# One decoder step on one core: halves of gate weight tiles multiplied in pairs, a router computed by tokens, another order of the first loads, and a last norm in quarters

## The chip, the cores and the metric

The kernel runs on one core of one Trainium2 chip, in one launch. The metric is the device time in microseconds (us) of an execution; lower is better. TensorE is called PE here (and its weight loads PEld), VectorE DVE, ScalarE ACT, GpSimd POOL, SyncE SP.

## The reference

One inference step of a two-layer decoder for 272 prompt tokens (16 of them meta tokens) and 8 samples of 8 new tokens, 336 tokens in all, 1024 features, float32.

```
for l in range(2):
    z = rmsnorm(x) @ w_in[l]            # q, k, v, recurrent x and y, two merge gates
    att = window attention with sinks(q, k, v)
    xc = conv4(xr)                      # 1280 recurrent features, 16 blocks of 80
    r = sigmoid(xc_block @ w_a + b_a);  i = sigmoid(xc_block @ w_i + b_i)
    rec = RG-LRU(r, i, xc) * gelu(yr)
    x += (sigmoid(ga) * (att @ w_att_proj) + sigmoid(gr) * (rec @ w_rec_proj)) @ w_out
    x += swiglu(rmsnorm(x))             # layer 0: dense; layer 1: top 2 of 8 experts by a router
return rmsnorm(x), and the new caches and states
```

The two gates `r` and `i` multiply the 1280 features by a block-diagonal matrix of sixteen 80x80 blocks. Cut into 128x128 tiles, such a matrix has 13 tiles that aren't zero in each half of 640 features: five on the diagonal, and eight beside it, which a block reaches by crossing a tile's border. A tile beside the diagonal holds weights in its first or in its last 64 rows alone.

## The kernel before

**Split products.** Activations lie features first, in tiles of 128 features x tokens. Every large product is made of three TensorE products of reduced-precision float32 (fp32r): high weights by high activations, high by low, low by high (`three`, lines 1492 to 1494). Weights stream in chunks of eight 128x128 tiles (512 KB) by the queue of SP into a ring of four buffers `raw`; ACT (`hi`) or DVE (`hi_lo`, line 941) copies a chunk to `whi`, and DVE writes what is left to `wlo` (`lo`, line 935). A buffer is loaded again when PE has counted the chunk up in `pe_chunk`. A chunk of 24 products is `chunk`.

**Start.** PE first runs 11 filler products on zeros (line 1518, `N_WARM[0]`). `par` (gains) and the two halves of chunk 0 are loaded by ACT's queue, `x` by SP's. ACT makes `xuh` (`high`, line 567) and the halves of `whi`, DVE `xul` (`low`, line 946) and the halves of `wlo` (line 1028), in turns. POOL adds up seven sums of squares (line 411), which PE needs at the end of chunk 3 (line 1499).

**Gates.** After attention come eight chunks, a pair for each gate and half: the first chunk of a pair holds tiles for the outputs i = 0, 1, 2, the second those for 3, 4 (`GATE_IN` lists each output's input tiles). Output i is summed in PSUM bank 2+i over 360 columns. DVE meanwhile splits the next chunks (`hi_lo`) and does the last convolution (`conv(9)`); ACT takes the outputs from PSUM by a sigmoid (line 713), after a sigmoid over merge gates of its own (line 705), when `pe_chunk` says that their chunk is done. PE waits on `gate_evac` before it writes a bank again. After them come 10 chunks of the recurrent `y` (`C_Y`), 8 of the attention projection (`C_A`); there DVE has hi_lo, lo, squares, scans and copies, behind a multiplication that waits for all gate outputs (line 1171).

**Router.** In the last eight chunks of layer 1, `feature(k)` follows each chunk: one float32 product gives 64 rows (8 experts and room for the sum of squares) x 336 tokens (`wr64`, line 1691), and three transposes put the features in token order. After `feature(7)` DVE copies the logits, PE transposes them, ACT takes the norm's root (line 849), and DVE picks the experts. PE runs `keep_clock` products on data that nobody reads in the waits (`N_WARM[1:]`, line 1755). POOL gathers the first expert's rows, PE transposes them (`turn_rows`, line 1783), ACT copies them (`high_rows`), and the experts' products begin (lines 1792 to 1796).

**Last norm.** PE sums squares over features into two groups of 64 rows x 168 tokens, ACT takes the root, DVE the reciprocal, PE spreads it over 128 rows, DVE scales, SP stores.

## Time and profile before

| | |
|---|---|
| time, median of 3 runs | 1368.62 us (1368.56 to 1371.15) |
| profiled execution: its own time | 1368.22 us |
| its span | 1366.4 us |
| PE, PEld busy | 99%, 92% |
| DVE, ACT, POOL busy | 79%, 59%, 10% |
| granted TensorE clock, mean | 0.997 |

The rows below are of that one execution. Each row of a timeline gives the start, the duration, the engine, the line, the operation with its output and inputs, and in brackets how long the engine was idle before it and what ended that. "x6" means six like instructions, with their whole time. A float32 product appears as two passes.

### The profile page before, as it was taken

To read this page: it belongs to the slowest core of one execution; us is meant where nothing else is said; L and a number is where in the kernel's file an instruction comes from. 1 tells how busy PE (TensorE), PEld (TensorE's weight loads), DVE (VectorE), ACT (ScalarE), POOL (GpSimd) and SP (SyncE) were. 2 spreads that over 40 slices of the span, in tenths; PEclk is the share of its full clock that TensorE was granted. 3 is DMA by queue.
4 is the path that set the end of the run, shared out by engine and by line. 5 is a ranking of instruction groups with operands and counts; after the bars stand their busy time and mean duration, and the time that the engine had idled before them with its cause. 6 is when DMAs were issued, how large, how long until landed. Compare 5 with 4: busy or idle time off the path is not lost.

```text
span 1366.4 us, 23816 instructions
## 1 busy us (share of the span) xinstructions
PE 1349.9 (99%) x8300; PEld 1251.7 (92%) x8300; DVE 1079.2 (79%) x1641; ACT 808.6 (59%) x1215; POOL 139.2 (10%) x137
## 2 busy tenths in 40 slices
PE   8999999999999999999999999999999999999997
PEld 8999999999999999999989999987888888888886
DVE  5869988876666664456699899758999999999987
ACT  5455668325333333343666584257888888888885
POOL 3200003002000000001000030022012022022010
PEclk9999999999999999999999999999999999999999
DMA  6533344445444444444423444497999999999991
GB/s 240 165 128 99 109 144 148 146 140 175 153 138 143 146 142 139 144 141 148 157 94 108 144 150 151 158 363 301 409 396 396 399 383 376 397 386 375 398 348 57
DMA packets 83401, 298.31 MB, mean 218 GB/s; under 512 B 9584, under 2 KB 10864, under 8 KB 83312
## 3 DMA queue, kind: packets, MB, share of 16 engines
q1 hardware_dynamic: 77472, 277.73, 57.2%
q0 software_dynamic: 5408, 18.72, 4.6%
q8 instruction: 57, 0.93, 0.3%
q10 hardware_dynamic: 432, 0.66, 0.1%
q14 instruction: 32, 0.26, 0.1%
HBM read 285.50 MB, written 11.58 MB: 217 GB/s over the span
## 4 chain that ended last, share of the span: by engine, by line
PE 90%; DVE 7%; ACT 2%; issue 1%; DMA 0%; ACTq 0%; DVEq 0%
PE ps L1492 19%; PE ps L1494 18%; PE ps L1493 18%; PE ps L1792 10%; PE ps L1796 10%; PE ps L1793 10%; DVE wlo L935 1%; PE ps L1828 1%; PE ps L1592 1%; DVE mx L1097 1%; ACT sp L627 1%; DVE sp L1093 1%; DVE xc L1074 1%; DVE sp L1108 0%; PE ps L1608 0%
## 5 line engine op out<-in xcount | busy, mean ns | idle before, releaser
L935 DVE TENSOR_TENSOR wlo<-raw,whi 128x1024 fp32r<-128x1024 f32 x231 | 285.7, 1238 | 122.0 <-ACT whi L549 113.8
L1014 DVE TENSOR_TENSOR mwlo<-mraw,mwhi 128x1024 fp32r<-128x1024 f32 x290 | 343.9, 1222 | 30.0 <-ACT mwhi L549 25.2
L549 ACT ACTIVATE mwhi<-mraw 128x1024 fp32r<-128x1024 f32 x290 | 304.3, 1061 | 60.6 <-PE ps L1796 55.9
L549 ACT ACTIVATE whi<-raw 128x1024 fp32r<-128x1024 f32 (+1 forms) x207 | 216.9, 1050 | 193.2 <-DMA raw<-w_mix 118.9
L1492 PE MATMUL ps<-xuh,whi 128*128 128x336 f32 x576 | 183.7, 319 | 2.5 <-DVE wlo L1028 2.0
L1493 PE MATMUL ps<-xul,whi 128*128 128x336 f32 x576 | 182.0, 316 | 0.0
L1494 PE MATMUL ps<-xuh,wlo 128*128 128x336 f32 x576 | 181.7, 315 | 0.0
L1492 PE MATMUL ps<-xnh,whi 128*128 128x336 f32 (+1 forms) x544 | 174.0, 320 | 1.9 <-DVE wlo L935 1.8
L1494 PE MATMUL ps<-xnh,wlo 128*128 128x336 f32 (+1 forms) x544 | 170.7, 314 | 0.0
L1493 PE MATMUL ps<-xnl,whi 128*128 128x336 f32 (+1 forms) x544 | 170.6, 314 | 0.0
L1792 PE MATMUL ps<-mwhi,xeh 128*128 128x512 f32 x384 | 152.7, 398 | 0.4 <-ACT xeh L549 0.4
L1796 PE MATMUL ps<-mwhi,xel 128*128 128x512 f32 x384 | 149.9, 390 | 0.0
L1793 PE MATMUL ps<-mwlo,xeh 128*128 128x512 f32 x384 | 149.6, 390 | 0.0
L1492 PEld LDWEIGHTS ps<-xuh,whi 128*128 128x128 f32 x576 | 108.7, 189 | 3.3 <-DVE wlo L1028 2.3
L1493 PEld LDWEIGHTS ps<-xul,whi 128*128 128x128 f32 x576 | 108.9, 189 | 0.3
L1492 PEld LDWEIGHTS ps<-xnh,whi 128*128 128x128 f32 x544 | 102.2, 188 | 7.4 <-issue 5.7
L1494 PEld LDWEIGHTS ps<-xuh,wlo 128*128 128x128 f32 x576 | 108.8, 189 | 0.0
L1493 PEld LDWEIGHTS ps<-xnl,whi 128*128 128x128 f32 x544 | 102.4, 188 | 0.0
L1494 PEld LDWEIGHTS ps<-xnh,wlo 128*128 128x128 f32 x544 | 102.2, 188 | 0.0
L1796 PEld LDWEIGHTS ps<-mwhi,xel 128*128 128x128 f32 x384 | 72.1, 188 | 15.8 <-DVE xel L1413 0.4
L1792 PEld LDWEIGHTS ps<-mwhi,xeh 128*128 128x128 f32 x384 | 72.2, 188 | 14.5 <-issue 0.6
L1793 PEld LDWEIGHTS ps<-mwlo,xeh 128*128 128x128 f32 x384 | 72.2, 188 | 14.0
(323 smaller groups left out, 2621.7 us busy)
## 6 DMA issues: line engine op xcount, KB each, us to landing
mraw<-w_moe SPq DMA_DIRECT2D x292, 512.0 KB, 8.1
raw<-w_mix SPq DMA_DIRECT2D x159, 512.0 KB, 3.6
raw<-w_ffn SPq DMA_DIRECT2D x72, 512.0 KB, 3.5
x<-x_in SPq DMA_DIRECT2D x4, 336.0 KB, 5.4
tok_d<-xt POOLq DMA_DIRECT2D x6, 224.0 KB, 4.3
ysum_d<-zero POOLq DMA_DIRECT2D x3, 448.0 KB, 10.7
ysum<-ysum_d POOLq DMA_DIRECT2D x3, 448.0 KB, 10.5
o_y<-nt SPq DMA_DIRECT2D x8, 168.0 KB, 1.9
```

Source lines behind the costliest of these rows:

```text
L549: return nc.scalar.activation(out, in_, ACT.Copy)
L627: nc.scalar.activation(sp[q][:, i * w:(i + 1) * w], sp[q][:, i * w:(i + 1) * w], ACT.Exp, bias=neg[q][:, i:i + 1], accum_out=rsum[q][:, i: ...
L935: v.tensor_tensor(wlo[c % RING][:, :, :], raw[c % RING][:, :].rearrange("p (k n) -> p k n", n=P), f32(whi[c % RING][:, :, :]), ALU.subtrac ...
L1014: v.tensor_tensor(mwlo[q % MRING][:, :, :], mraw[q % MRING][:, :].rearrange("p (k n) -> p k n", n=512), f32(mwhi[q % MSPLIT][:, :, :]), AL ...
L1074: step(v.scalar_tensor_tensor(out=xc[:, t, :], in0=ext[:, t, j:j + C], scalar=w[:, KR * j + t:KR * j + t + 1], in1=xc[:, t, :], op0=ALU.mu ...
L1093: ins = v.scalar_tensor_tensor(out=sp[q][:, g * per:(g + 1) * per], in0=ps[2 + 2 * q + g][:, 0:per], scalar=HD ** -0.5, in1=mask[:, 0:per] ...
L1492: mm(out, wh, xh, start=start, stop=False)
L1493: mm(out, wh, xl, start=False, stop=False)
L1494: return mm(out, wl, xh, start=False, stop=stop)
L1792: mm(out, lhs_h, hi[:, n, :], start=start, stop=False)
L1793: mm(out, lhs_h, lo[:, n, :], start=False, stop=False)
L1796: return mm(out, lhs_l, hi[:, n, :], start=False, stop=stop)
```

## The change

The gates: each pair of chunks is now one block. The five diagonal tiles are multiplied as before (`gate_in`). The eight tiles beside the diagonal are multiplied over 64 rows each (`gate_edges`), in turns one on rows 0 to 63 and one on rows 64 to 127, into different banks. A pair's first chunk is counted up in `pe_chunk` three pairs of half products before the second. The start: half a chunk, the first tile of `x`, the other half and the second tile go first on SP's queue; ACT takes a root (and so loads its table) before anything arrives; chunk 1 is split by halves. The router: `by_tokens` makes the tokens the rows, with 9 columns for each third of the tokens, in place of the 64-row product, so that the copy and the transposes of the logits fall away. The first expert's rows are copied by ACT ahead of one weight chunk. The filler counts change. The last norm works on four groups of 32 rows x 84 tokens.

```diff
-N_WARM = (11, 7, 3, 20)
+N_WARM = (11, 15, 7, 16)
...
+GATE_SLOT = {(i, k): n for part in ((0, 1, 2), (3, 4)) for n, (i, k) in enumerate((i, k) for i in part for k in GATE_IN[i])}
...
-            for q in range(4):
+            sy.dma_start(raw[0][:, 0:512], w_mix[0, 0, :, 0:512]).then_inc(raw_half, 16)
+            sy.dma_start(x[:, 0:1, :], x_in[:, 0:1, :]).then_inc(x_first, 16)
+            sy.dma_start(raw[0][:, 512:CH], w_mix[0, 0, :, 512:CH]).then_inc(raw_loaded[0], 16)
+            sy.dma_start(x[:, 1:2, :], x_in[:, 1:2, :]).then_inc(x_loaded[0], 16)
+            for q in range(1, 4):
                 sy.dma_start(x[:, 2 * q:2 * q + 2, :], x_in[:, 2 * q:2 * q + 2, :]).then_inc(x_loaded[q], 16)
...
-            def first_hi(h):
-
-                act.wait_ge(raw_half if h == 0 else raw_loaded[0], 16)
-                copy(whi[0][:, 4 * h:4 * h + 4, :], raw[0][:, 512 * h:512 * h + 512].rearrange("p (k n) -> p k n", n=P))\
+            def first_hi(c, h):
+
+                act.wait_ge(raw_half if c == 0 and h == 0 else raw_loaded[c], 16)
+                copy(whi[c][:, 4 * h:4 * h + 4, :], raw[c][:, 512 * h:512 * h + 512].rearrange("p (k n) -> p k n", n=P))\
                     .then_inc(hi_half if h == 0 else hi_done, 1)
 
             act.dma_start(par[:, :, :], par_in).then_inc(par_loaded, 16)
-            act.dma_start(raw[0][:, 0:512], w_mix[0, 0, :, 0:512]).then_inc(raw_half, 16)
-            act.dma_start(raw[0][:, 512:CH], w_mix[0, 0, :, 512:CH]).then_inc(raw_loaded[0], 16)
+            act.wait_ge(eps_set, 1)
+            nc.scalar.activation(rms3[:, 0:1], eps[:, :], ACT.Sqrt)
+            first_hi(0, 0)
             high(0, 0)
-            first_hi(0)
             high(0, 1)
-            first_hi(1)
+            first_hi(0, 1)
             for k in range(2, KD):
                 high(0, k)
-            hi(1)
+            first_hi(1, 0)
+            first_hi(1, 1)
             square(0, 0)
             square(0, 1)
             hi(2)
...
-                    for q in range(N_NEXT, LEAD):
-                        mhi(q, r)
+                    mhi(N_NEXT, r)
+                    mhi(N_NEXT + 1, r)
                     high_rows(0, 0, r)
                     high_rows(0, 1, r)
+                    for q in range(N_NEXT + 2, LEAD):
+                        mhi(q, r)
...
-            nc.scalar.activation(esg[:, 0:T // 2], ps[0][:, 0:T // 2], ACT.Sqrt, bias=eps[:, :], scale=1.0 / D).then_inc(rms_done, 1)
+            nc.scalar.activation(esg[:, 0:T // 4], ps[0][:, 0:T // 4], ACT.Sqrt, bias=eps[:, :], scale=1.0 / D).then_inc(rms_done, 1)
...
+            first_lo(0, 0)
             low(0, 0)
-            first_lo(0)
             low(0, 1)
-            first_lo(1)
+            first_lo(0, 1)
             for k in range(2, KD):
                 low(0, k)
-            lo(1)
+            first_lo(1, 0)
+            first_lo(1, 1)
...
-            ve.wait_ge(router_mm, 1)
-            v.tensor_copy(lgt[0:9, :], ps[7][0:9, 0:T]).then_inc(logits_t, 1)
...
-                for j in range(N_G):
-                    c = c0 + C_G + j
-                    half, part, pair = j // 4, j % 2, j // 2
+                def gate_in(c, i, k, half, start=False, stop=False):
+
+                    slot = GATE_SLOT[i, k]
+                    return three(ps[2 + i][:, 0:C], whi[c % RING][:, slot, :], wlo[c % RING][:, slot, :], xch[:, 5 * half + k, :],
+                                 xcl[:, 5 * half + k, :], start, stop)
+
+                def gate_edges(low, high, half):
+
+
+                    for n in range(3):
+                        for rows, (c, i, k, start, stop) in ((slice(0, 64), low), (slice(64, P), high)):
+                            slot, t = GATE_SLOT[i, k], 5 * half + k
+                            w, xin = (wlo if n == 2 else whi)[c % RING], xcl if n == 1 else xch
+                            ins = mm(ps[2 + i][:, 0:C], w[rows, slot, :], xin[rows, t, :], start=start and n == 0, stop=stop and n == 2)
+                    return ins
+
+                for pair in range(N_G // 2):
+                    c, half = c0 + C_G + 2 * pair, pair // 2
                     pe.wait_ge(lo_done, c + 1)
-                    slot = 0
-                    for i in ((3, 4) if part else (0, 1, 2)):
-                        pe.wait_ge(xc_split, KR * l + 5 * half + GATE_IN[i][-1] + 1)
+                    for i in range(3):
+                        pe.wait_ge(xc_split, KR * l + 5 * half + i + 1)
                         if pair:
                             pe.wait_ge(gate_evac, 20 * l + 5 * (pair - 1) + i + 1)
-                        for k in GATE_IN[i]:
-                            t = 5 * half + k
-                            ins = three(ps[2 + i][:, 0:C], whi[c % RING][:, slot, :], wlo[c % RING][:, slot, :], xch[:, t, :],
-                                        xcl[:, t, :], k == GATE_IN[i][0], k == GATE_IN[i][-1])
-                            slot += 1
-                    ins.then_inc(pe_chunk, 1)
+                        gate_in(c, i, i, half, start=True)
+                    pe.wait_ge(lo_done, c + 2)
+                    pe.wait_ge(xc_split, KR * l + 5 * half + 5)
+                    gate_edges((c, 0, 1, False, True), (c, 1, 0, False, False), half)
+                    if pair:
+                        pe.wait_ge(gate_evac, 20 * l + 5 * (pair - 1) + 4)
+                    gate_edges((c, 2, 3, False, False), (c + 1, 3, 2, True, False), half).then_inc(edges_mm, 1)
+                    gate_in(c + 1, 3, 3, half)
+                    if pair:
+                        pe.wait_ge(gate_evac, 20 * l + 5 * pair)
+                    gate_in(c + 1, 4, 4, half, start=True)
+                    pe.wait_ge(edges_mm, N_G // 2 * l + pair + 1)
+                    gate_edges((c, 1, 2, False, True), (c, 2, 1, False, True), half).then_inc(pe_chunk, 1)
+                    gate_edges((c + 1, 3, 4, False, True), (c + 1, 4, 3, False, True), half).then_inc(pe_chunk, 1)
...
+                def by_tokens(features, weights, stop=False):
+
+                    for t in range(NT):
+                        ins = mm(ps[7][0:TR, 9 * t:9 * t + 9], features[:, TR * t:TR * t + TR], weights, start=False, stop=stop and t == NT - 1)
+                    return ins
+
                 def feature(k):
 
+                    if k == 0:
+                        mm(ps[7][0:TR, 0:9 * NT], zero[:, 0:TR], zero[:, 0:9 * NT], start=True, stop=False)
                     pe.wait_ge(x_added, 16 + k + 1)
-                    mm(ps[7][0:64, 0:T], wr64[:, k, :], x[:, k, :], start=k == 0, stop=False)
+                    by_tokens(x[:, k, :], wr9[:, k, :])
...
-            mm(ps[7][0:64, 0:T], e64[:, :], acc3[:, :], start=False, stop=False)
+            by_tokens(acc3[:, :], e9[:, :])
             feature(KD - 1)
             pe.wait_ge(sq_done, KD * 4)
-            mm(ps[7][0:64, 0:T], e64[:, :], ssq[(KD - 1) % 2][:, :], start=False, stop=True).then_inc(router_mm, 1)
-            pe.wait_ge(tok_a, NT)
-            pe.wait_ge(logits_t, 1)
-            for t in range(NT):
-                ins = nc.tensor.transpose(ps[3][0:TR, 9 * t:9 * t + 9], lgt[0:9, TR * t:TR * t + TR], ident[0:9, 0:9])
-            ins.then_inc(logits_mm, 1)
+            by_tokens(ssq[(KD - 1) % 2][:, :], e9[:, :], stop=True).then_inc(logits_mm, 1)
...
-                for h in range(2):
-                    ins = mm(ps[0][64 * h:64 * h + 64, 0:T // 2], ones[:, 0:64], sq[:, k, T // 2 * h:T // 2 * h + T // 2],
+                for h in range(4):
+                    ins = mm(ps[0][32 * h:32 * h + 32, 0:T // 4], ones[:, 0:32], sq[:, k, T // 4 * h:T // 4 * h + T // 4],
                              start=k == 0, stop=k == KD - 1)
...
-            for h in range(2):
-                ins = mm(ps[1][:, T // 2 * h:T // 2 * h + T // 2], ident[:, 64 * h:64 * h + 1].to_broadcast([P, P]), rstd[:, 0:T // 2], start=True, stop=True)
+            for h in range(4):
+                ins = mm(ps[1][:, T // 4 * h:T // 4 * h + T // 4], ident[:, 32 * h:32 * h + 1].to_broadcast([P, P]), rstd[:, 0:T // 4], start=True, stop=True)
```

The data, `wr9` and `e9` (9 columns in place of 64), and the ring stay otherwise as they are.

ACT's first instructions, before and then after the change (`raw0` is the first ring buffer, `rms3` takes the early root):

```order
L588 DMA par_191<-par_in 128x264
L589 DMA raw0_50<-w_mix 128x512
L590 DMA raw0_50<-w_mix 128x512
L567 ACT_TABLE_LOAD [waits par_loaded]
L567 ACTIVATE xuh_92<-x_49,par_191 128x336 [waits x_loaded0]
L549 ACTIVATE whi0_58<-raw0_50 128x512 [waits raw_half]
L567 ACTIVATE xuh_92<-x_49,par_191 128x336 [waits x_loaded0]
L549 ACTIVATE whi0_58<-raw0_50 128x512 [waits raw_loaded0]
```

```order
L594 DMA par_190<-par_in 128x264
L596 ACT_TABLE_LOAD
L596 ACTIVATE rms3_242<-eps_206 128x1 [waits eps_set]
L555 ACTIVATE whi0_58<-raw0_50 128x512 [waits raw_half]
L573 ACTIVATE xuh_92<-x_49,par_190 128x336 [waits par_loaded,x_first]
L573 ACTIVATE xuh_92<-x_49,par_190 128x336 [waits x_loaded0]
L555 ACTIVATE whi0_58<-raw0_50 128x512 [waits raw_loaded0]
L573 ACTIVATE xuh_92<-x_49,par_190 128x336 [waits x_loaded1] x2
```

The table load no longer stands behind the wait for `par`, and the first half of `whi` stands ahead of the first `xuh`.

PE in the second pair of gate chunks of layer 0, before (the outputs i = 1 and the first tile of i = 2) and then after the change (from the diagonal tile of i = 2 on):

```order
L1492 MATMUL ps3<-xch_73,whi2_60 128x360 [waits gate_evac,xc_split]
L1493 MATMUL ps3<-xcl_74,whi2_60 128x360
L1494 MATMUL ps3<-xch_73,wlo2_56 128x360
L1492 MATMUL ps3<-xch_73,whi2_60 128x360
L1493 MATMUL ps3<-xcl_74,whi2_60 128x360
L1494 MATMUL ps3<-xch_73,wlo2_56 128x360
L1492 MATMUL ps3<-xch_73,whi2_60 128x360
L1493 MATMUL ps3<-xcl_74,whi2_60 128x360
L1494 MATMUL ps3<-xch_73,wlo2_56 128x360
L1492 MATMUL ps4<-xch_73,whi2_60 128x360 [waits gate_evac,xc_split]
```

```order
L1498 MATMUL ps4<-xch_73,whi2_60 128x360 [waits gate_evac,xc_split]
L1499 MATMUL ps4<-xcl_74,whi2_60 128x360
L1500 MATMUL ps4<-xch_73,wlo2_56 128x360
L1661 MATMUL ps2<-xch_73,whi2_60 128x360 [waits xc_split,lo_done]
L1661 MATMUL ps3<-xch_73,whi2_60 128x360
L1661 MATMUL ps2<-xcl_74,whi2_60 128x360
L1661 MATMUL ps3<-xcl_74,whi2_60 128x360
L1661 MATMUL ps2<-xch_73,wlo2_56 128x360
L1661 MATMUL ps3<-xch_73,wlo2_56 128x360
L1661 MATMUL ps4<-xch_73,whi2_60 128x360 [waits gate_evac]
L1661 MATMUL ps5<-xch_73,whi3_61 128x360
```

The products of line 1661 take 64 rows each and alternate between two banks; the wait for the pair's second chunk (`lo_done`) now stands behind nine products instead of 24.

PE at the end of the router, before and then after the change (`acc3` and `ssq1` are sums of squares, `xg` the scaled features):

```order
L1742 MATMUL ps7<-acc3_186,e64_180 64x336 [waits acc_done]
L1691 MATMUL ps7<-x_49,wr64_179 64x336 [waits x_added]
L1696 MATMUL ps5<-cst_190,xg1_183 112x128 [waits xg_done]
L1696 MATMUL ps6<-cst_190,xg1_183 112x128
L1696 MATMUL ps2<-cst_190,xg1_183 112x128
L1745 MATMUL ps7<-ssq1_95,e64_180 64x336 [waits sq_done]
L1749 MATMUL ps3<-cst_190,lgt_178 112x9 [waits logits_t,tok_a]
L1749 MATMUL ps3<-cst_190,lgt_178 112x9 x2
L1755 MATMUL ps1<-mwhi0_154,onesr_239 128x512 [waits x_added]
```

```order
L1719 MATMUL ps7<-e9_179,acc3_185 112x9 [waits acc_done]
L1719 MATMUL ps7<-e9_179,acc3_185 112x9 x2
L1719 MATMUL ps7<-wr9_178,x_49 112x9 [waits x_added]
L1719 MATMUL ps7<-wr9_178,x_49 112x9 x2
L1732 MATMUL ps5<-cst_189,xg1_182 112x128 [waits xg_done]
L1732 MATMUL ps6<-cst_189,xg1_182 112x128
L1732 MATMUL ps2<-cst_189,xg1_182 112x128
L1719 MATMUL ps7<-e9_179,ssq1_95 112x9 [waits sq_done]
L1786 MATMUL ps1<-mwhi0_154,onesr_238 128x512 [waits x_added]
```

Three products of 9 columns stand where one of 336 stood, and the transposes of `lgt` are gone.

## Rows read from the trace of the kernel before

**Rows 1.** The page: engines busy, and DMA in 40 slices.

```profile
PE 1349.9 (99%) x8300; PEld 1251.7 (92%) x8300; DVE 1079.2 (79%) x1641; ACT 808.6 (59%) x1215; POOL 139.2 (10%) x137
DMA  6533344445444444444423444497999999999991
```

**Rows 2.** The timeline of the first 25 us.

```profile
4.94 1.28 ACT L567 ACT_TABLE_LOAD   x1 [4.94 <-DMA par<-par_in]
7.40 0.68 DVE L1028 TENSOR_TENSOR wlo<-raw,whi 128x512 fp32r<-128x512 f32 x1
9.20 2.96 DVE L946 SCALAR_TENSOR_TENSOR xul<-x,par,xuh 128x336 fp32r<-128x336 f32 x6
9.81 0.65 PE L1492 MATMUL ps<-xuh,whi 128*128 128x336 f32 x1 [0.47 <-DVE xul L946]
14.50 8.71 POOL L411 TENSOR_TENSOR acc<-acc,ssq 128x336 f32<-128x336 f32 x6
24.71 0.73 PE L1499 MATMUL ps<-acc,cst 128*128 128x336 f32 x2
```

**Rows 3.** Windows: busy PE, PEld, DVE, ACT, POOL, granted clock, DMA.

```profile
10.00:12.00 2.00, 2.00 (x8) 2.00 (x9) 2.00 (x5) 2.00 (x4) 1.05 (x2) 0.50 1.04 423
173.13:198.85 25.72, 25.72 (x160) 25.72 (x157) 22.27 (x28) 15.82 (x28) 0.00 (x0) 1.00 0.51 151
198.90:265.10 66.20, 66.20 (x432) 66.20 (x431) 60.28 (x86) 45.72 (x67) 14.81 (x11) 1.00 0.47 151
```

**Rows 4.** The timeline of PE: attention scores, products over 64 rows.

```profile
79.20 0.31 PE L1494 MATMUL ps<-xnh,wlo 128*128 128x336 f32 x1
79.45 0.72 PE L1563 MATMUL ps<-qkx 64*128 64x128 f32 x8
80.35 0.32 PE L1493 MATMUL ps<-xnl,whi 128*128 128x336 f32 x1
116.21 1.14 PE L1568 MATMUL ps<-qkx 64*128 64x256 f32 x8
```

**Rows 5.** The timeline of DVE in the gates, layers 0 and 1.

```profile
182.41 0.69 DVE L941 CAST whi<-raw 128x1024 fp32r<-128x1024 f32 x1
200.23 2.03 DVE L1171 TENSOR_TENSOR ig<-ig,xc 128x1800 f32<-128x1800 f32 x1 [1.62 <-ACT ig L713]
768.33 0.69 DVE L941 CAST whi<-raw 128x1024 fp32r<-128x1024 f32 x1
785.13 2.03 DVE L1171 TENSOR_TENSOR ig<-ig,xc 128x1800 f32<-128x1800 f32 x1 [1.68 <-ACT ig L713]
```

**Rows 6.** The timeline of ACT at the gates' end, layer 0.

```profile
198.06 0.77 ACT L705 ACTIVATE gates<-gates 128x672 f32<-128x672 f32 x1
199.18 1.01 ACT L713 ACTIVATE ig<-ps,par 128x360 f32<-128x360 f32 x2 [0.35 <-PE ps L1494]
```

**Rows 7.** The loads of `raw` between 165 and 230 us.

```profile
DMA to landing us min/median/max: 3.4/3.5/3.9
```

**Rows 8.** The timeline in the attention projection: DVE layer 0, PE layer 1.

```profile
237.35 1.23 DVE L935 TENSOR_TENSOR wlo<-raw,whi 128x1024 fp32r<-128x1024 f32 x1
823.07 0.41 PE L1492 MATMUL ps<-atth,whi 128*128 128x320 f32 x1 [0.37 <-DVE wlo L935]
```

**Rows 9.** The timeline from the router's end to the first expert.

```profile
920.74 0.73 PE L1691 MATMUL ps<-x,wr 128*64 128x336 f32 x2
921.98 1.57 ACT L549 ACTIVATE xt<-ps 112x512 f32<-112x512 f32 x3 [1.45 <-PE ps L1696]
933.67 0.86 PEld L1783 LDWEIGHTS ps<-cst,xe 128*128 128x128 f32 x8 [0.41 <-DMA xe<-tok_d,idx]
934.45 1.06 ACT L549 ACTIVATE xeh<-ps 128x512 fp32r<-128x512 f32 x2
```

**Rows 10.** The timeline of the last norm.

```profile
1356.16 1.28 ACT L911 ACT_TABLE_LOAD   x1
1357.99 1.20 DVE L1480 RECIPROCAL rstd<-esg 128x168 f32<-128x168 f32 x1 [2.24 <-ACT esg L911]
```

43 lines of the change are left out of this document (21 added, 22 removed).

## The prediction

> **What bounds the kernel now.** I read the page first: PE is busy 99% of the span [rows 1]. So a saving must shorten PE's stream or end one of its few waits, and what is saved elsewhere is hidden. Then I read the timeline stage by stage at the five places touched.
>
> At the start PE waits for data: `par` lands at 4.94 and ACT then loads a table for 1.28 before it does anything; the first chunk's third tile starts at 9.81, released by DVE's `xul`, and PE is then at half clock [rows 2, 3]. In the gates, 25.72 hold 156 products, 0.165 each, without a wait; the 18 chunks after them take 66.20, 3.68 a chunk or 0.153 a product of 336 columns [rows 3]. Close behind PE runs DVE: in the projection after the gates it ends a `wlo` at 237.35 + 1.23 = 238.58, and PE, 11 chunks after 198.90, takes it at 198.90 + 40.46 = 239.36, only 0.8 later. In layer 1 PE does wait there, 0.37 [rows 3, 8]. So behind the gates a gain of PE lasts only as far as DVE comes earlier too. That sets the main term.
>
> **The start.** The table load moves under the load of `par`, and the first half of `whi` can be ready when `par` lands. DVE can start at about 4.95 instead of 6.92, which is 9.81 less the 2.9 of its five steps (xul and wlo in turns). PE's third tile comes at about 7.85 instead of 9.81. Two more things follow. PE's idle time between the fillers and the first product shrinks, so I take it that the clock isn't lowered; DVE's 0.49 a tile (2.96 for 6) then paces the chunk: its eighth tile at 7.85 + 5 x 0.49 = 10.3, its end at 10.8. By halves, chunk 1 starts 0.68 after DVE's last `xul`, at 11.1. Before, chunk 1 must have started at 24.71 - 2 x 3.68 - 3.22 = 14.1. That would be 3.0. But POOL's seven sums take 7 x 1.45 = 10.1 and can't start before two squares on ACT, at about 11.7: PE gets them at 21.9 instead of at 24.71, 2.8 earlier [rows 2, 3]. What hides SP's three more DMA issues is that bytes, not issues, set the landings. Term: **-2.8**. Bounds: -1.3, if the clock falls as before; -3.2.
>
> **The gates on PE.** A pair of chunks had 39 products. Now 15 are whole and 24 are halves. Do two halves run side by side? The scores have such a pattern in float32: eight passes of 64 rows and 256 columns end within 1.14 [rows 4]. A float32 pass of 336 columns takes about 0.28 (two in 0.73, the last with its tail [rows 9]), so 256 take 0.21, and eight in a row would take 1.7. They run in pairs. The switch costs: from 79.20 + 0.153 to 80.35 - 0.153 are 0.84 for eight passes of 128 columns, which in pairs need 4 x 0.107 = 0.43; 0.42 remain for a way there and back [rows 4]. A pair of chunks has two such ways: 15 x 0.165 + 12 x 0.165 + 0.84 = 5.30 instead of 6.43. Four pairs would save 4.5 a layer.
>
> The Trainium skill, "TensorEngine Tiling (Array Packing)", Key Properties, says that a change of tiling mode drains TensorE. By that rule there is a cost beside the saved products, and the trace agrees (0.42).
>
> **The gates on DVE.** DVE isn't moved by this. In layer 0 it starts `whi` of the third pair's first chunk at 182.41, 9.28 after the gates' start at 173.13, and needs 0.7 + 1.23 for the two steps: ready at 11.2. PE would be there at 10.7, so it waits 0.5. The pair's second chunk follows 1.9 later, at 13.1, but PE asks for it after nine products, at 12.7: 0.4 more. The third pair ends at 16.9, the fourth, whose chunks (freed at 10.2 and 10.8, 3.5 to land [rows 7]) are split by 15.9 and 17.8, at 22.35. PE ends the gates 25.7 - 22.35 = 3.35 earlier [rows 3, 5].
>
> Behind that: `pe_chunk` of a pair's first chunk now comes near the pair's end, so after the last pair ACT still has three outputs, the merge sigmoid and two outputs (5 x 0.45 + 0.77, less 0.3 that lie before PE's end: 2.75) instead of two outputs (1.3) [rows 6]. DVE's multiplication starts at 22.35 + 2.75 = 25.1 instead of 27.1 [rows 5]: DVE moves by 1.9 only. With its 0.8 lead less a few tenths in later chunks, PE keeps about **-2.5** in layer 0.
>
> In layer 1 the multiplication at 785.13 stands, as in layer 0, 27.1 after the gates' start, which is then 758.0; the `whi` step at 768.33 is 10.3 after it, a microsecond later than in layer 0 [rows 5]. By the same steps the gates end at 23.35, DVE's multiplication starts at 26.1 instead of 27.1 after the start, and PE has no lead to spend (it waits already [rows 8]): **-0.9**. Together **-3.4**. Bounds: -1.8, if a switch costs 0.6; -5.0 at 0.2.
>
> **The router.** A 64-row product of two passes took 0.73 with its tail, about 0.66 of PE's time [rows 9]. `by_tokens` issues three products of two passes; their columns are few, so six weight loads set the price: 0.103 each by [rows 9] (0.86 for 8), 0.064 by the 64-row passes of [rows 4] (0.72 for 8, less the tail). I take 0.48, between: 0.18 saved for each of features 0 to 5, less a zero product, is 0.9. At the end three such products stand before the transposes, 0.55; the copies of 1.57 on ACT move by that, and the root stands right behind them. DVE's copy and the logits' transposes lay beside these copies and give nothing more. The first expert's rows, at 934.45 behind three weight chunks, come 0.25 earlier behind two [rows 9]. The gather's flight stays. More fillers (8 x 0.23 = 1.9 if uncovered; 512 columns by the 0.153) end before the mask is ready; the last block, four shorter, ends before the gather lands. Term: **-1.7**; bounds 0 and -3.3.
>
> **The last norm.** The sums were hidden by ACT's table load until 1356.16 + 1.28, so they give 0.1. The reciprocal halves from 1.20 to about 0.68 (6 ns a column, as 168 to 84 asks), the root loses 0.07, and spreading by eight passes instead of four costs 0.15 more [rows 10]. Term: **-0.5**; bounds -0.1 and -1.0.
>
> **Sum.** 1368.22 - 2.8 - 3.4 - 1.7 - 0.5 = 1359.8, against a profiled execution 0.4 below the median of the runs (1368.62). I forecast **1359.8**.
>
> **Rivals.**
> *The clock falls at the start as before.* Half clock stood from about 9.9 to 13.1; PE still has short gaps in the first tiles. It gives back 1.5: 1361.3.
> *Weight loads fill the slot.* Each half product needs a load. If it costs 0.103 as a full one does [rows 9], a slot of two halves takes 0.206, not 0.165: 0.5 more a pair, the gates give 1.9, in all 1361.3. Against it: 64-row loads in [rows 4] take at most 0.064 to 0.09.
> The Trainium skill, "TensorE: Matmul & The Clock Gate", section LDWEIGHTS, says that a load costs its columns, not its rows, 107 ns for 128 columns. By that rule this rival would hold, with a slot of 0.21, an estimate; the scores' rows speak against it.
> *DVE isn't the limit.* If DVE's and ACT's order leaves PE its whole 4.5 a layer, the sum is 1368.2 - 5.0 - 9.0 = 1354.2. The 0.37 wait in [rows 8] speaks against it.
> *The transfers of the expert stage set its pace.* DMA is at 9 tenths there [rows 1]. Then all earlier gains vanish in it: 1367.7. Against it: no wait of PE there is on a transfer.
> *Halves hinder each other.* In fp32r, unlike float32, two halves might run one after another, each with its load exposed: 0.10 + 0.165 for each, 0.53 a slot, 4.4 more a pair of chunks, 35 in all: 1368 + 35 - 9 = 1394. It loses from a slot of about 0.28 on, where the gates cost the 5.0 that the rest gains. The overlap in [rows 4] speaks against it.
>
> **How the numbers follow.** Forecast 0.55, clock 0.13, loads 0.10, DVE no limit 0.08, transfers 0.05, halves hinder 0.05, anything else 0.04. The likeliest case by itself runs from 1357.5 to 1362 by its bounds; with the next two cases and part of the third the range is 1355.5 to 1365.5. A measurement of this kernel tells about 0.2%, 2.7, from no change. Faster: the first four cases and half of the rest, 0.88; the same: 0.06; slower: 0.06.
>
> **What would show it.** Right: no half clock between 8 and 20; a chunk pair of 5.3 in the gates; two half products starting within 0.165; a wait of PE on `wlo` of about 0.5 before the third pair; DVE's multiplication more than 2 behind PE's last gate product; first expert product about 1.7 closer to the router's chunks. Wrong: a slot over 0.2, a switch over 0.6, a new wait of PE on `gate_evac` above 0.1 a pair, or `xe` waited for longer after the shorter filler block.

## The result, and the profile after

The changed kernel takes **1359.12 us** (median of 4 runs, 1358.95 to 1359.34) against 1368.59 us of the kernel before in the same comparison: a ratio of **0.9927**, 95% interval 0.9914 to 0.9941. The forecast was 1359.8 us, faster. The profiled execution takes 1359.04 us with a span of 1357.2 us, 9.2 less than before.

The page of the changed kernel, busy times and the chain that ended last:

```profile
PE 1339.0 (99%) x8383; PEld 1238.5 (91%) x8383; DVE 1077.4 (79%) x1641; ACT 806.5 (59%) x1215; POOL 138.6 (10%) x137
PE 83%; DVE 13%; ACT 2%; issue 1%; DMA 1%; SPq 0%; DVEq 0%; ACTq 0%
```

PE has 10.9 us less work than in [rows 1], but the span shrinks by 9.2: the rest came back as waits. The chain points the same way: DVE stood for 7% of it before and stands for 13% now.

The starts of a few instructions, in the timelines of both profiles, cut the span into pieces whose differences add up to the 9.2:

| piece, by PE's products | before | after | gained | forecast |
|---|---|---|---|---|
| start to the first sum of squares | 24.71 | 22.29 | 2.4 | 2.8 |
| layer 0, gates (first `xch`) to first `rech` | 92.34 | 89.29 | 3.05 | 2.5 |
| layer 1, the same | 90.16 | 88.96 | 1.20 | 0.9 |
| from there to the transposes of feature 7 | 73.20 | 71.02 | 2.2 | 0.9 |
| from there to the first expert product | 13.75 | 13.81 | -0.1 | 0.8 |
| from there to the first `nt` of the last norm (DVE) | 424.97 | 424.57 | 0.4 | 0.5 |

(`xch` and `rech` are the upper parts of the split inputs of the gates and of the recurrent projection; 18 chunks lie between the two.) The three pieces that are left out, from the sum of squares to the gates of layer 0, from `rech` to the gates of layer 1, and from `nt` to the end, differ by 0.03 or less.

**The start.** Timeline of the changed kernel, to compare with [rows 2]:

```profile
1.20 1.28 ACT L596 ACT_TABLE_LOAD   x1 [1.20 <-PEq L2083]
3.93 0.63 ACT L555 ACTIVATE whi<-raw 128x512 fp32r<-128x512 f32 x1 [1.24 <-DMA raw<-w_mix]
6.27 0.58 ACT L573 ACTIVATE xuh<-x,par 128x336 fp32r<-128x336 f32 x1 [1.24 <-DMA x<-x_in]
8.62 0.42 PE L1498 MATMUL ps<-xuh,whi 128*128 128x336 f32 x1 [0.39 <-DVE xul L953]
13.42 7.96 POOL L417 TENSOR_TENSOR acc<-acc,ssq 128x336 f32<-128x336 f32 x6 [0.46 <-ACT ssq L578]
22.29 0.73 PE L1505 MATMUL ps<-acc,cst 128*128 128x336 f32 x2
```

The table load is out of the way at 2.48 and the first half of the weights is split from 3.93. But ACT is idle from 5.02 to 6.27, for the transfer of the second `x` tile. So the third tile comes to PE at 8.62 instead of the forecast 7.85.

**The gates.** Windows of the changed kernel, with the columns of [rows 3]: the first chunk, the gates of layer 0, the 18 chunks behind them, the gates of layer 1:

```profile
8.00:12.00 4.00, 3.61 (x22) 3.10 (x21) 4.00 (x9) 4.00 (x10) 2.20 (x3) 1.00 1.03 412
170.70:192.85 22.15, 21.09 (x160) 17.29 (x156) 20.42 (x27) 13.66 (x25) 0.00 (x0) 1.00 0.49 166
192.92:259.50 66.58, 66.41 (x431) 66.12 (x430) 61.84 (x88) 47.37 (x71) 14.81 (x11) 1.00 0.48 153
752.59:775.80 23.21, 21.16 (x160) 17.30 (x156) 21.45 (x29) 13.49 (x25) 0.00 (x0) 1.00 0.46 160
```

The same number of products fills 22.15 where it filled 25.72. PE's timeline shows how, from the last whole product over twelve half products (two to a row) to the next whole one:

```profile
172.12 0.33 PE L1500 MATMUL ps<-xch,wlo 128*128 128x360 f32 x1
172.38 0.43 PE L1661 MATMUL ps<-xch,whi 64*128 64x360 f32 x2
172.65 0.32 PE L1661 MATMUL ps<-xcl,whi 64*128 64x360 f32 x2
172.82 0.32 PE L1661 MATMUL ps<-xch,wlo 64*128 64x360 f32 x2
...
173.30 0.32 PE L1661 MATMUL ps<-xch,wlo 64*128 64x360 f32 x2
173.56 0.43 PE L1498 MATMUL ps<-xch,whi 128*128 128x360 f32 x1
173.83 0.32 PE L1499 MATMUL ps<-xcl,whi 128*128 128x360 f32 x1
```

From 172.65 to 172.82 a pair of halves takes 0.165, as much as one whole product. A switch shows as 172.38 after 172.12 (0.26, not 0.165) and 172.65 after 172.38 (0.27): 0.20 for the way there, and again 0.20 for the way back, 0.40 in all.

At the end of the gates, the timeline of ACT and DVE in layer 0, against [rows 5, 6]:

```profile
194.55 1.02 ACT L718 ACTIVATE ig<-ps,par 128x360 f32<-128x360 f32 x2
195.60 2.04 DVE L1179 TENSOR_TENSOR ig<-ig,xc 128x1800 f32<-128x1800 f32 x1 [1.07 <-ACT ig L718]
```

PE's waits over the whole span (in all, how many, the longest):

```profile
PE ps L1498 <- DVE wlo L942: 5.0, 9, 1.4
PE ps L1498 <- ACT rg L718: 1.0, 4, 0.3
```

The multiplication starts 24.9 after the gates' start (27.1 before), and PE waits for `wlo` 5.0 us in nine waits (2.1 in four before). Four waits of 0.25 on ACT's outputs, two a layer, are new.

**The router and the last norm.** Timelines of the changed kernel, against [rows 9] and [rows 10]:

```profile
901.67 0.31 PE L1500 MATMUL ps<-mgh,wlo 128*128 128x320 f32 x1
901.82 0.66 PE L1719 MATMUL ps<-wr,x 128*112 128x9 f32 x6
902.33 0.52 PE L1732 MATMUL ps<-cst,xg 128*112 128x128 f32 x3
924.96 1.09 PE L1814 MATMUL ps<-cst,xe 128*128 128x128 f32 x8 [1.24 <-DMA xe<-tok_d,idx]
1347.40 1.28 ACT L918 ACT_TABLE_LOAD   x1
1349.05 0.68 DVE L1486 RECIPROCAL rstd<-esg 128x84 f32<-128x84 f32 x1 [2.07 <-ACT esg L918]
```

The reciprocal takes 0.68, as forecast. The first expert's transposes now wait 1.24 for the gather; in [rows 9] their weight loads waited 0.41.

### The profile page after: what moved, and what is told of

The parts are those of the page before. It is cut to its first block, busy times and chain, and to the rows that moved or that the text cites. A ratio compares the mean times of both kernels' runs of the same rounds, so it can differ in the third digit from the quotient of the medians.

```text
span 1357.2 us, 23976 instructions
## 1 busy us (share of the span) xinstructions
PE 1339.0 (99%) x8383; PEld 1238.5 (91%) x8383; DVE 1077.4 (79%) x1641; ACT 806.5 (59%) x1215; POOL 138.6 (10%) x137
## 4 chain that ended last, share of the span: by engine, by line
PE 83%; DVE 13%; ACT 2%; issue 1%; DMA 1%; SPq 0%; DVEq 0%; ACTq 0%
PE ps L1498 16%; PE ps L1500 16%; PE ps L1499 16%; PE ps L1823 10%; PE ps L1827 10%; PE ps L1824 10%; DVE wlo L942 4%; DVE xc L1082 2%; DVE whi L948 1%; DVE mx L1105 1%; DVE sp L1101 1%; PE ps L1859 1%; DVE xcl L1087 1%; PE ps L1661 1%; PE ps L1814 0%
```

## The experiments

Two things must be known for reading them. First, the kernel before is not one number: in each comparison its executions fall into two groups, 1367.8 to 1368.7 and 1370.3 to 1371.7, so that its median is 1368.4 to 1370.9. The lowest time is 1367.8 in four of the five. I therefore read ratios within a comparison, and stage times of the profiles. Second, how well stage times repeat. The changed kernel, unedited, in a second comparison:

> The changed kernel once more, unedited, on the chip and against the runs of the three edits sent with it, since the kernel before takes 1368.6 us on one chip and 1370.9 on another. Every theory expects a ratio to the kernel before of 0.991 to 0.993; the span and the stage times of its profile show how far two executions of one kernel differ (0.3 us a stage is expected).

It took 1360.75 us (1359.28 to 1361.66, 5 runs), ratio 0.9938 (0.9925 to 0.9952). Its two layers took 89.30 and 88.97, against 89.29 and 88.96, and two later profiles with unedited layers (x1_first, fillers_before) lie within 0.04 of these. So the layers' times repeat far better than whole times. The ends of the span don't: the first sum of squares came at 21.94 instead of 22.29, and from the first expert product to the first `nt` it took 425.45 instead of 424.57. A row of PE's timeline and a window of the last norm, with the columns of [rows 3], show where the 0.9 went:

```profile
1349.14 2.00 PE L1977 MATMUL ps<-rstd,cst 128*128 128x84 f32 x8 [2.00 <-DVE rstd L1486]
1348.00:1351.00 3.00, 1.86 (x8) 1.78 (x8) 0.68 (x1) 0.37 (x2) 0.00 (x0) 0.65 0.00 0
```

PE waited 2.00 for the reciprocal, the granted clock fell to half in that wait, and the eight passes behind it took 2.00 instead of the 1.12 of the first profile, where the clock stayed at 1.00 until PE was done.

**Do the parts add up?** The changed kernel with the old gate products (the whole block of `gate_in` and `gate_edges` goes back to the loop over `N_G` chunks):

> The changed kernel with the gate products of before. Theory (the parts add up): 4.2 us more than the changed kernel, 1363.3. Rival (the parts lean on each other, as when an earlier start only moves a wait): the gain without the gates is not 5.0 but well below.

1363.37 us (1362.8 to 1365.69, 6 runs), ratio 0.9955 (0.9944 to 0.9967). Its layers took 92.34 and 90.15, the numbers of the kernel before.

The kernel before with the new gate products alone:

> The kernel before with the changed gate products alone (its start, router and last norm as before). Theory, the parts add up and the overlapped halves are the gain: in the changed kernel the gates gave 3.05 us in layer 0 and 1.20 us in layer 1, so this kernel is 4.2 us faster than the one before, ratio 0.9969 (0.996 to 0.998). Rival, the gates' gain depends on the earlier start (other phase of the weight ring, the split of chunk 1 at the start): under 2.5 us, ratio 0.998 or more.

1365.48 us (1363.78 to 1365.71, 5 runs), ratio 0.996 (0.9946 to 0.9974). Its layers took 89.32 and 88.94: the gates gain 3.0 and 1.2, wherever the rest of the kernel stands. The rival, that their gain hangs on the new start, falls. Its span, 1363.7, is only 2.7 below that of the kernel before, because the clock fell once more in this execution, behind a wait of PE near the first expert: from the last transposes of the router to the first expert product it took 1.4 more.

**Is it the overlap?** The changed kernel with its half products over all 128 rows. The other 64 rows of such a tile hold zeros, so the sums stay the same, and so do the order, the buffers and the number of products.

```diff
-                        for rows, (c, i, k, start, stop) in ((slice(0, 64), low), (slice(64, P), high)):
+                        for rows, (c, i, k, start, stop) in ((slice(0, P), low), (slice(0, P), high)):
```

> The changed kernel, but each product beside the diagonal takes all 128 rows (the other 64 are zeros), in the same order and with the same waits, so that none can run side by side and no switch of tiling is left. Theory (the gain is the overlap of two halves): a pair of chunks takes 39 slots of 0.165 = 6.4 instead of 5.3; with ACT's later outputs behind the last pair, layer 0 loses 3.6 and layer 1 2.6: 6.2 us more than the changed kernel, 1365.3. Rival (order and waits gave the gain): within 1 us of the changed kernel.

1364.44 us (1364.14 to 1369.01, 5 runs), ratio 0.9962 (0.9949 to 0.9975), against 0.9927 for the changed kernel: 4.8 slower by the ratios. PE's timeline of this run:

```profile
175.52 0.49 PE L1661 MATMUL ps<-xch,whi 128*128 128x360 f32 x2
175.84 0.49 PE L1661 MATMUL ps<-xcl,whi 128*128 128x360 f32 x2
176.18 0.50 PE L1661 MATMUL ps<-xch,wlo 128*128 128x360 f32 x2
177.51 0.33 PE L1498 MATMUL ps<-xch,whi 128*128 128x360 f32 x1
```

Two take 0.335 now, one after another, and the switch is gone (175.52 comes 0.17 after the whole product at 175.35). Layer 0 takes 92.92 and layer 1 91.15, 3.6 and 2.2 more than in the changed kernel, and 0.6 and 1.0 more than before the change. So the gates' gain is the overlap; the new order without it loses a little.

**What takes back part of it behind the gates?** The changed kernel with DVE's multiplication behind the gates cut to 8 of 1800 columns, which leaves most of the gated input of one half undone:

```diff
-                v.tensor_tensor(ig[:, 5:KR, :], ig[:, 5:KR, :], xc[:, 5:KR, :], ALU.mult).then_inc(xc_used, 1)
+                v.tensor_tensor(ig[:, 5:6, 0:8], ig[:, 5:6, 0:8], xc[:, 5:6, 0:8], ALU.mult).then_inc(xc_used, 1)
```

> The changed kernel, with DVE's multiplication behind all gate outputs (2.03 us, the second half of the input gate by the convolution) cut to 8 columns of one tile, so part of the gated input is left out. Theory (DVE's chain behind the gates takes back part of what PE gains there): PE ended the gates 3.6 and 2.6 us sooner than before but kept 3.05 and 1.20; with DVE 2 us earlier it keeps it all: 2 us less than the changed kernel, 1357.1. Rival (PE sets the pace there): no change, 1359.1.

1357.78 us (1357.0 to 1358.48, 5 runs), ratio 0.9909 (0.9896 to 0.9922). Layers: 88.83 and 88.02, 0.46 and 0.94 less than the changed kernel. What could be won back is known from the traces: the 18 chunks from the gates' end to `rech` take 67.07 in layer 0 (66.49 before the change) and 65.70 in layer 1 (64.32 before), 0.6 and 1.4 more. The short multiplication gives 1.4 of these 2.0 back. Could the same cut have helped the kernel before as well? In layer 0 it could not: PE has no idle time behind the gates there, and the changed kernel has this, where short_mult again has none:

```profile
215.63 0.39 PE L1498 MATMUL ps<-xnh,whi 128*128 128x336 f32 x1 [0.17 <-DVE wlo L942]
```

In layer 1 PE waits for `wlo` behind the gates once in the kernel before (0.37), three times in the changed one (0.52, 0.28, 0.37) and twice in short_mult (0.15, 0.36). So DVE behind the gates takes back part of PE's gain, as the prediction's theory has it. What short_mult doesn't give back is 0.1 a layer for the way out of the half products, and in layer 1 the wait of 0.15 with what hangs on it.

If so, DVE's work can be moved. First, ACT's sigmoid over merge gates behind the gate outputs in the odd pairs, where DVE waits for them:

```diff
-                    nc.scalar.activation(gates[:, 2 * j:2 * j + 2, kept(l)], ...Sigmoid).then_inc(gates_ready, 1)
+                    if j % 2 == 0:
+                        merge_sigmoid()
...
+                    if j % 2:
+                        merge_sigmoid()
```

> The changed kernel, with ScalarE's sigmoid over the merge gates of the odd pairs put behind the five gate activations of that pair instead of ahead of them. Theory, the end of each gates stage is VectorE's last multiplication, which waits for ScalarE's last activation behind that sigmoid (0.66 us): the multiplication ends some 0.5 us earlier in each layer, 0.8 to 1.0 us in all, and TensorE's waits on gate_evac (0.25 each) shrink; 1358.1 us, ratio to the kernel before 0.992. Rival, the chain is TensorE's and VectorE's weight splits alone: no difference from the changed kernel (within 0.2 us); and if the later sigmoid holds back the scan's inputs, slower.

1359.2 us (1357.75 to 1359.24, 4 runs), ratio 0.9913 (0.9898 to 0.9928). Its timeline, with all five outputs in one row of ACT:

```profile
192.67 2.37 ACT L721 ACTIVATE ig<-ps,par 128x360 f32<-128x360 f32 x5 [1.86 <-PE ps L1666]
194.90 0.79 ACT L711 ACTIVATE gates<-gates 128x672 f32<-128x672 f32 x1
195.07 2.03 DVE L1184 TENSOR_TENSOR ig<-ig,xc 128x1800 f32<-128x1800 f32 x1 [0.25 <-ACT ig L721]
```

The multiplication starts 24.25 after the gates' start instead of 24.90, and the layers take 88.87 and 88.44, 0.42 and 0.52 less, as expected. The whole time doesn't show it: this execution lost 0.5 again at the transposes of two router features, before one of which PE waits 0.20 for ACT's copy `xt`, and 0.6 in the last norm, where the clock fell over the spreading passes (1.70 instead of 1.12).

Second, three of eight upper parts a layer from DVE to ACT:

```diff
+                    if j in (2, 4, 6):
+                        act.wait_ge(lo_done, c + 2)
+                        hi(c + 2)
...
-                    hi_lo(c0 + C_G + j + 2)
+                    (lo if j in (2, 4, 6) else hi_lo)(c0 + C_G + j + 2)
```

> The changed kernel, with the upper parts of three of the eight gate chunks of each layer made by ScalarE instead of VectorE. Theory, TensorE's waits for the lower parts of the gate weights (5.0 us in all over 9 waits in the changed kernel, 2.1 before) are VectorE's load, so most of those within the gates stages go: 1.0 to 1.8 us faster than the changed kernel, about 1357.7. Rival, the waits lie behind transfers or the end of the stage lies with ScalarE's activations, which now come later: no gain, or 0.5 to 1.5 us slower than the changed kernel.

1358.44 us (1357.75 to 1359.4, 4 runs), ratio 0.9911 (0.9896 to 0.9926). Layers: 89.27 and 88.23, so nothing in layer 0 and 0.73 in layer 1, less than the 1.0 to 1.8 expected. The gain is at PE's wait for `wlo` ahead of the third pair, which went from 1.43 to 0.73.

Both together:

> The changed kernel with the odd merge sigmoids behind the gate activations and three upper parts a layer on ScalarE, the x tiles' transfers as in the changed kernel. Each edit alone shortened its stages in the trace (0.42 and 0.52 us; 0.02 and 0.73 us). Theory, both add up inside the layers, and the layers' gain reaches the end: 1.2 to 1.7 us faster than the changed kernel. Rival, what is gained in the layers is taken back between the layers' end and the last experts, where transfers and not the engines set the time, or ScalarE is now the late one: within 0.4 us of the changed kernel.

**1357.59 us** (1357.41 to 1359.63, 5 runs), ratio 0.9922 (0.9908 to 0.9936), beside 1360.75 and 0.9938 for the changed kernel on the same chip. Layers: 88.76 and 87.75, 0.54 and 1.22 less than the unedited kernel's there: about the sums of the two edits, 0.42 + 0.02 and 0.52 + 0.73. The intervals of the ratios overlap, so the whole time alone doesn't settle it. The stage times settle it for layer 1: two more kernels with the same edits (together and start_fill, below) took 87.72 and 87.73 there. Layer 0 took 89.21 and 88.89 in them, so its gain is anything from 0.1 to 0.5.

**The start.** The second `x` tile's transfer ahead of the second half of the first weight chunk:

```diff
+            sy.dma_start(x[:, 1:2, :], x_in[:, 1:2, :]).then_inc(x_loaded[0], 16)
             sy.dma_start(raw[0][:, 512:CH], w_mix[0, 0, :, 512:CH]).then_inc(raw_loaded[0], 16)
-            sy.dma_start(x[:, 1:2, :], x_in[:, 1:2, :]).then_inc(x_loaded[0], 16)
```

> The changed kernel with the transfer of the second x tile issued ahead of that of the second half of the first weight chunk. Theory from the changed kernel's trace, the second tile landed at 6.27 because it was issued fourth, 0.47 us behind its place: it lands 0.3 to 0.5 us earlier and the first sums of squares come at 22.0, 0.3 earlier. Rival, the half chunk is then what is late: it holds up ScalarE's queue and all tiles behind it, and the first sums come at 23 or later (they came at 24.13 in the kernel with three edits), 1 to 2 us slower.

1360.08 us (1358.64 to 1361.74, 4 runs), ratio 0.9937 (0.9922 to 0.9952): the same as the unedited kernel. ACT takes the second tile right behind the first, at about 5.1 (5.94 and 6.27 in two profiles of the changed kernel); the third tile reaches PE at 7.98 instead of 8.29 and 8.62; the sums come at 21.87, against 21.94 and 22.29. So the tile landed earlier in this execution, but a gain at the sums isn't shown: in the profiles with the unedited start and no fall of the clock there they come anywhere from 21.89 to 22.78. The short 0.4 of the start's term has no place of its own either: the second profile of the same code has 2.8.

All three edits at once:

> The changed kernel with three edits at once: the odd merge sigmoids behind the gate activations, three upper parts a layer on ScalarE, and the second x tile's transfer ahead of the second half of the first weight chunk. Theory, they work at different places and add up: 0.9 + 1.4 + 0.3 = 2.6 us faster than the changed kernel, 1356.5 us, ratio to the kernel before 0.9911. Rival, the first two both unload the same chain (VectorE's end of the gates), so that together they give no more than the larger alone: about 1357.5; or ScalarE becomes late and takes it all: 1359 or more.

1358.9 us (1358.16 to 1360.03, 4 runs), ratio 0.9913 (0.9898 to 0.9928). Its layers took 89.21 and 87.72, but its profile has the sums at 24.13, 1.8 late. The edit alone didn't do that (x1_first, with the same start, had them at 21.87). In this execution the second and third tiles came to ACT at 5.82 and 7.95 instead of 5.13 and 6.75, PE waited 1.39 for the third, and then the clock fell, which leads to the next question.

**Where does the scatter come from?** [rows 3] show half a clock at the start of the kernel before. There are twelve profiles of the changed kernel and its variants. In three of them it fell in the first tiles (full_rows, together, fillers_before), in two around the first expert (fillers_before, start_fill), in six in the last norm before its spreading was done (full_rows, together and fillers_before again, and after_again, short_mult, sigmoid_later); behind PE's last product it is down in all twelve. Windows of full_rows, of the first chunk:

```profile
8.00:12.00 4.00, 3.02 (x10) 2.67 (x11) 3.64 (x8) 4.00 (x9) 1.44 (x2) 0.50 1.03 411
```

And of fillers_before, described below, of the first chunk and of the router's end:

```profile
8.00:12.00 4.00, 3.83 (x15) 3.40 (x15) 4.00 (x9) 4.00 (x10) 2.19 (x3) 0.57 1.03 411
920.00:925.00 5.00, 4.80 (x13) 3.42 (x12) 3.29 (x23) 2.26 (x4) 1.05 (x1) 0.50 0.20 50
```

Their sums came at 25.55 and 23.47. At each fall in the first tiles PE had been waiting for `xul`: 2.0 in one wait in full_rows (the fall came inside it), 0.7 and 0.9 in fillers_before. To fill these waits, the kernel sig_hi with three more products of zeros:

```diff
-N_WARM = (11, 15, 7, 16)
+N_WARM = (12, 15, 7, 16)
...
+                    if c == 0 and k in (1, 2):
+                        mm(ps[7][:, 0:P], zero[:, :], zero[:, :], start=True, stop=True)
```

> The kernel sig_hi with three more products of zeros at the start: twelve instead of eleven ahead of TensorE's first chunk, and one each ahead of the second and third k tile of that chunk, where TensorE waits for xul (0.33 to 2.0 us in the traces so far). Theory, executions of one kernel differ by up to 2 us or more because the granted clock falls to half at 8 to 12 us in some of them (0.57 and 0.50 in two profiles, where the sums of squares came at 23.5 and 25.6 instead of 22), after such a wait, and the added products, about 0.4 us each, lie inside the waits: the clock keeps 1.00 up to 16 us, the sums of squares come at 22.0 to 22.4, and all executions lie within 0.5 us of 1357.5. Rival, the scatter comes from somewhere else, such as the transfers: executions scatter by 2 us as before; or the added products delay the first chunk: 0.4 to 1.2 us slower than sig_hi.

1357.64 us (1357.33 to 1359.95, 5 runs), ratio 0.992 (0.9906 to 0.9933). In its profile the clock holds at the start, PE is busy without a gap from 4 to 16 us, and the sums come at 22.04; the added products cost nothing. But the five executions still fall into two groups, and the profiled one (1359.08) is of the slower. Its trace shows why. Its windows:

```profile
8.00:12.00 4.00, 4.00 (x25) 3.51 (x25) 3.94 (x8) 3.91 (x10) 2.22 (x4) 1.00 1.03 415
925.00:930.00 5.00, 5.00 (x15) 3.76 (x16) 5.00 (x6) 3.52 (x5) 0.00 (x0) 0.66 0.99 390
```

PE's timeline of the same run behind the gather:

```profile
923.45 1.09 PE L1824 MATMUL ps<-cst,xe 128*128 128x128 f32 x8 [1.45 <-DMA xe<-tok_d,idx]
924.87 0.49 PE L1833 MATMUL ps<-mwhi,xeh 128*128 128x512 f32 x1 [0.33 <-ACT xeh L555]
...
926.54 0.63 PE L1834 MATMUL ps<-mwlo,xeh 128*128 128x512 f32 x1
```

After 1.45 of waiting for the gather the clock fell, at 0.43 from product to product instead of 0.23, and 1.5 us were lost between the transposes and the end. So the forecast that all executions would agree falls: there is more than one such place, and filling the first is not enough. That the added products are what held the clock at the start isn't shown by this one profile, since it held in most others too.

**The router's fillers.** The changed kernel with the filler counts of before, `N_WARM = (11, 7, 3, 20)`:

> The changed kernel with the numbers of filler products around the router as before (7, 3 and 20 in place of 15, 7 and 16). Theory, the fillers lie in waits of TensorE (for VectorE's gates of the router and then for the transfer of xe) and the clock stays at full speed with either: the first expert's transposes start within 0.2 us of the changed kernel's, the time is the same within 0.5 us. Rival, with fewer fillers the granted clock falls in the router's waits: windows of half the clock between 912 and 925 us and 1 us or more lost; or the 16 in place of 20 is what let the transposes start earlier, then 0.5 to 1 us slower.

1361.03 us (1360.66 to 1363.44, 4 runs), ratio 0.9939 (0.9924 to 0.9954). PE's timeline:

```profile
918.65 0.27 PE L1791 MATMUL ps<-msk,trir 112*112 112x24 f32 x1 [1.88 <-DVE msk L1353]
921.57 7.02 PE L1786 MATMUL ps<-mwhi,onesr 128*128 128x512 f32 x20
928.43 1.03 PE L1814 MATMUL ps<-cst,xe 128*128 128x128 f32 x8
```

PE waits 1.88 for the mask, the clock falls, and the 20 fillers take 7.02; at full clock 16 take 3.90. They end so late that PE takes the gathered rows without a wait: the transposes start 7.52 after the product of line 1801 (5.46 in the changed kernel), 2.0 lost. This execution shows the rival right. With the old counts the clock fell near the first expert in gates_only2 too, but not in the profile of the kernel before; with the new counts it fell there in one profile of eleven (start_fill). The medians differ by 0.3 only, the lowest times by 1.4 (1360.66 against 1359.28), so how often it happens isn't settled.

## Why the prediction was right, and where it wasn't

The number came out within 0.7 of the forecast, and part of that is luck: the terms missed by up to 0.85 and their errors partly cancel, and the second comparison of the same kernel gave a ratio of 0.9938 instead of 0.9927 and a median 1.6 us higher.

**The start, 2.8 forecast, 2.4 measured (2.8 in the second profile).** The chain was right: the table load out of the way, then DVE's turns, then POOL's sums, which start at 12.05 instead of the forecast 11.7. The step that fell short is the third tile at 7.85: it took the second tile of `x` to be there in time, but ACT was idle 1.24 for it. It was issued fourth on SP's queue, behind half a chunk of weights. The prediction's "bytes, not issues, set the landings" isn't what failed: the 16 DMA engines were busy all the while (a share of 0.99 from 5.00 to 6.20), so the half chunk's bytes ahead of the tile held it up. How much that cost isn't settled: with the tile ahead of the half chunk it came to ACT at 5.13 in x1_first, but at 5.82 in together. The rival of a falling clock is real, though not the usual case: it happened in three of twelve profiles, and their sums came 1.2 to 3.3 later (23.5 to 25.6 against 22.3), where 1.5 was forecast. Part of that is tiles that landed late, 7.75 instead of 6.27 for the second one in full_rows.

**The gates, 3.4 forecast, 4.25 measured.** The slot of two halves is 0.165, and the two ways of a pair of chunks cost 0.40 each where 0.42 was read from [rows 4]. PE ended the gates 22.2 and 23.3 after their start (22.35 and 23.35 forecast), DVE's multiplication began at 24.9 (25.1). The wait ahead of the third pair, forecast at 0.5 in layer 0 and a microsecond more in layer 1, was 0.4 and 1.43. The term was too small in its last step: PE's gain in the gates was 3.6 and 2.6, and what DVE took back behind them was 0.6 and 1.4, where the prediction took 0.9 and 1.5 from 3.35 and 2.4. The rival "DVE isn't the limit" falls: it needed 4.5 a layer, and moving DVE's work (sig_hi, short_mult) won 1.4 to 1.8 back. The new waits on `gate_evac` (0.25, four of them) are the sign that the text had named as wrong; they are real, small, and were left out of the sum.
The Trainium skill, "TensorEngine Tiling (Array Packing)", Key Properties, says that tiles run independently and that a change of mode drains TensorE. The trace agrees with both: 0.165 for two halves, 0.20 for each switch.
The Trainium skill's rule of 107 ns for a load of 128 columns ("TensorE: Matmul & The Clock Gate", LDWEIGHTS) is for one load; the slot of 0.21 that the prediction made of it needs two loads one after the other. They lie side by side in this trace, two in the 0.19 that the page of the profile gives for one load of 128 rows:

```profile
172.66 0.19 PEld L1661 LDWEIGHTS ps<-xch,wlo 64*128 64x128 f32 x2
```

**The router, 1.7 forecast, 2.1 measured, but not from where the prediction had it.** The features gave 2.2 instead of 0.9, the end nothing instead of 0.8. A feature with its chunk takes 4.39 instead of 4.69, 0.30 less. 0.20 of it is `by_tokens`, 0.51 to the next product instead of 0.71 (0.18 forecast); the other 0.1 is a step that the prediction left out: PE comes later to the 64-column product than to one of 112 columns, likely because it was itself a switch of tiling. The six steps from feature 0 to feature 6 give 1.7, the product of zeros takes what feature 0 gains, and from feature 6 to the transposes of feature 7, with sums of squares between them, it is 0.5. The kernel before, at such a place:

```profile
909.32 0.31 PE L1494 MATMUL ps<-mgh,wlo 128*128 128x320 f32 x1
909.56 0.78 PE L1691 MATMUL ps<-x,wr 128*64 128x336 f32 x2
910.27 0.54 PE L1696 MATMUL ps<-cst,xg 128*112 128x128 f32 x3
```

0.24 to the 64-column product, against 0.15 (901.67 to 901.82) to one of 112 columns. At the end, the root on ACT came only 0.26 earlier behind feature 7 (0.55 forecast), and the gather's flight, from POOL's issue to the transposes, took 4.45 instead of 4.10, which undid it. "More fillers end before the mask is ready" was right, and perhaps worth more than it said: with the old counts the clock fell in two of three profiles. The longer wait for `xe` was named as a sign of being wrong; it came with the gather's later landing, and the four fillers less cost nothing, since the last of the 16 ended at 923.72 and the rows landed at 924.96.

**The last norm, 0.5 forecast, 0.4 measured**, with the reciprocal at 0.68; spreading by eight passes cost 0.28, not 0.15. What the prediction had no term for is the clock: PE waits 2.00 for the reciprocal, 1.74 before, and in six of the twelve profiles the clock fell before the eight passes were done, which took back 0.4 to 0.9. In the two profiles with the old norm it didn't. So the 0.4 holds for executions without such a fall.

**The other rivals.** Weight loads don't fill the slot (0.165, not 0.206). The halves don't hinder each other; where they can't overlap (full_rows, 0.335 for two, but without the switches), the layers are 0.6 and 1.0 slower than before, and the other parts keep the kernel ahead. The prediction's bound for this rival was worked out wrongly: by its own terms the gates cost the 5.0 that the rest gains from a slot of 0.31 on, not 0.28. The transfers of the expert stage don't set its pace: all pieces before it reached the end, 424.57 against 424.97. So the gains were off by -0.4 (start), +0.85 (gates), +0.4 (router) and -0.1 (norm), which leaves 0.8: 9.2 where the sum had 8.4.

## What to carry to other kernels

Block-diagonal weights whose blocks cross tile borders leave half-empty tiles; two of these with different halves, in turns on rows 0 to 63 and 64 to 127 and into different banks, cost the time of one product, and 0.4 us more for each excursion out of the full tiling, so gather the halves in long runs. A narrow output tile in the middle of full ones costs some time too (0.24 instead of 0.15 until it starts) that doesn't show in its own duration. When PE is made faster, look at once at what follows behind it on DVE and ACT: here two rearrangements there bring the change's gain from 4.2 to 5.6 to 6.0 us in the two layers. Waits of PE of a microsecond or two cost more than themselves when the clock falls behind them. Whether filling them pays isn't shown: sig_hi and start_fill are the fastest versions run that compute everything, and they take the same (1357.59 and 1357.64). More fillers for the gather's wait, and any for the wait in the last norm, weren't tried.

## What the runs showed of the hardware

- The granted clock falls to half (1.2 GHz of 2.4) in some executions of one and the same code, after waits of PE of 0.7 to 2.0 us between products; in others, after waits of the same length, it doesn't (1.01 before the first product of the second run of the changed kernel, 1.27 for the gather in sig_hi, 2.00 for the reciprocal in the changed kernel, all at 1.00 behind it). Of the four variants of the changed kernel whose profile shows such a fall ahead of the last norm, the profiled execution was the slowest in three (full_rows, together, fillers_before) and the second slowest in one (start_fill). The other executions have no trace, but their mean granted clock is known, and it goes with the groups: of the 39 executions of the kernel before in the last four comparisons, the 18 up to 1368.7 have 0.997 or 0.998 (one 0.996), the 21 from 1370.3 on 0.994 to 0.996. So the slower group ran longer at half clock; where in the kernel isn't shown.
- At the start the profile can show a clock of 1.00 and products at half pace: 0.62 for the product at 5.99 in the changed kernel and 0.39 for the same product in its second profile, with passes on zeros of 0.42 and 0.28 just before.
- In fp32r two 64-row products over 360 columns, with their weight loads, run in the 0.165 us of one; a switch from 128-row to 64-row products or back costs 0.2.
